# Seven-product feed-forward sets: the last two products exchanged, operand splits in halves of the depth

## The reference, cut to what matters

```
x = x + 0.5 * swiglu_ffn(rmsnorm(x), ffn1 gate, up, down)
x = x + hybrid_mixer(rmsnorm(x), ...)
x = x + 0.5 * swiglu_ffn(rmsnorm(x), ffn2 gate, up, down)
x = rmsnorm(x)

def swiglu_ffn(x, w_gate, w_up, w_down):
    return (silu(x @ w_gate) * (x @ w_up)) @ w_down        # hidden width 2816
```

## Time and profile before

| | us |
|---|---|
| median of three runs | 1777.34 |
| profiled execution | 1777.71 |
| its span | 1775.9 |
| PE busy | 1721.1 (97%) |
| DVE busy | 1010.5 (57%) |
| ACT busy | 704.5 (40%) |
| PE waiting before a product of the seven-product sets (L1600) | 16.2, 14 times |

### The profile page before, as it was taken

How to read it: one execution, slowest core, us unless ns; L and a number is a source line. 1 busy time by engine, 2 the same in 40 slices (tenths; PEclk the granted TensorE clock), 3 DMA queues, 4 the chain that set the end, 5 groups by cost and what they waited for, 6 DMA issues and landing times.

```text
span 1775.9 us, 21351 instructions
## 1 busy us (share of the span) xinstructions
PE 1721.1 (97%) x8703; PEld 1277.9 (72%) x8703; DVE 1010.5 (57%) x1489; ACT 704.5 (40%) x1144; POOL 78.9 (4%) x78
## 2 busy tenths in 40 slices
PE   7999999998999999999999999999999999999998
PEld 6878888885454545454477788898877887788896
DVE  4768865643333333333457866765577457856765
ACT  4556435441111111111335445454355435545453
POOL 0000000000000000000001111100000001111100
PEclk9999999998999999999999999999999999999999
DMA  6222225547999999999947888883303167898781
GB/s 216 94 72 72 95 81 180 193 154 289 421 421 420 421 421 421 420 421 421 372 122 170 213 201 196 179 190 124 119 0 107 49 194 185 192 220 196 166 200 56
DMA packets 117512, 385.74 MB, mean 217 GB/s; under 512 B 7088, under 2 KB 22592, under 8 KB 91424
## 3 DMA queue, kind: packets, MB, share of 16 engines
q1 hardware_dynamic: 88928, 318.33, 46.7%
q0 software_dynamic: 26176, 61.78, 18.9%
q10 hardware_dynamic: 2304, 4.20, 0.6%
HBM read 364.36 MB, written 6.29 MB: 209 GB/s over the span
## 4 chain that ended last, share of the span: by engine, by line
PE 85%; DVE 9%; ACT 5%; issue 1%; DMA 0%; SPq 0%; DVEq 0%; ACTq 0%
PE PS L1491 12%; PE PS L1600 8%; PE PS L1602 8%; PE PS L1601 8%; PE PS L1524 6%; PE PS L1630 6%; PE PS L1632 6%; PE PS L1631 6%; PE PS L1634 3%; PE PS L1636 3%; PE PS L1635 3%; DVE lo L2386 2%; PE PS L1462 2%; PE PS L1463 2%; PE PS L1534 2%; PE PS L1708 2%
## 5 line engine op out<-in xcount | busy, mean ns | idle before, releaser
L2386 DVE TENSOR_TENSOR lo<-raw,hi 128x1024 fp32r<-128x1024 f32 (+2 forms) x273 | 328.1, 1232 | 199.1 <-ACT hi L1939 195.6
L1939 ACT CAST hi<-raw 128x1024 fp32r<-128x1024 f32 (+2 forms) x275 | 282.4, 1066 | 220.9 <-PE PS L1602 142.9
L1600 PE MATMUL PS<-hi,xh_ffn 128*128 128x512 f32 (+1 forms) x320 | 118.5, 370 | 6.3 <-issue 4.0
L1602 PE MATMUL PS<-hi,xl_ffn 128*128 128x512 f32 (+1 forms) x320 | 117.6, 368 | 0.0
L1601 PE MATMUL PS<-lo,xh_ffn 128*128 128x512 f32 (+1 forms) x320 | 117.5, 367 | 0.0
L1491 PE MATMUL PS<-raw,XG 128*64 128x512 f32 x352 | 117.1, 593 | 0.0
L2346 DVE TENSOR_TENSOR HF<-SG,PS 128x512 f32<-128x512 f32 x16 | 17.4, 1090 | 164.8 <-PE PS L1491 164.8
L2361 DVE SCALAR_TENSOR_TENSOR YL<-PS,SM,YH 128x512 fp32r<-128x512 f32 x30 | 21.1, 746 | 138.8 <-ACT YH L1922 138.8
L2369 DVE TENSOR_TENSOR x_sb<-x_sb,PS 128x512 f32<-128x512 f32 x128 | 78.2, 678 | 8.7 <-PE PS L1535 8.7
L1905 ACT COPY HT<-PS 128x512 f32<-128x512 f32 x16 | 9.4, 586 | 175.1 <-PE PS L1500 175.1
L1634 PE MATMUL PS<-xTh,hi 128*128 128x512 f32 x192 | 78.3, 408 | 0.4 <-DVE lo L2386 0.3
(11 more groups left out here) (520 smaller groups left out, 4237.5 us busy)
## 6 DMA issues: line engine op xcount, KB each, us to landing
raw<-in_w_in SPq DMA_DIRECT2D x26, 1024.0 KB, 5.1
rawz<-in_w_down_experts SPq DMA_DIRECT2D x25, 1024.0 KB, 10.9
raw<-in_w_up_experts SPq DMA_DIRECT2D x24, 1024.0 KB, 16.0
raw<-in_w_gate_experts SPq DMA_DIRECT2D x20, 1024.0 KB, 15.5
raw<-in_ffn_w_down SPq DMA_DIRECT2D x20, 1024.0 KB, 6.0
rawz<-in_w_up_experts SPq DMA_DIRECT2D x19, 1024.0 KB, 19.1
raw<-in_w_down_experts SPq DMA_DIRECT2D x16, 1024.0 KB, 12.0
rawz<-in_w_gate_experts SPq DMA_DIRECT2D x16, 1024.0 KB, 13.8
```

Source lines behind the costliest of these rows:

```text
L1600: e.matmul(o, xh[:, k, c], h[:, k, :], start=k == 0 and not more, stop=False, skip_group_check=more)
L1602: x = e.matmul(o, xl[:, k, c], h[:, k, :], start=False, stop=k == 3, skip_group_check=more)
L1939: e.copy(q.hi[:, a:b], q.raw[:, a:b]).then_inc(*a_hi((u, 0) if part == 0 else u))
L2386: e.tensor_tensor(q.lo[:, a:b], q.raw[:, a:b], q.hi[:, a:b].bitcast(F32), ALU.subtract).then_inc(*v_lo(key))
```

## The change

The last two products of a set change places: the lower left one (A22 on T4) is now the sixth and goes onto bank 4 (behind S3's), the end of the chain on bank 0 (S4 on the fourth block) is the seventh. So the hidden-end rows are complete after the sixth product and the hidden-top rows after the seventh; copy R0 (of bank 4 after product 1) takes the place of R4. The transposes of RB now stand before the next set's first product, with `hb` behind the seventh; those of SGT stand behind the next set's first product, with `ht` just ahead of them. The down set's left sums and splits are written at other products.

Every set is worked by halves of the depth. PE runs both row blocks on depths 0 and 1, then both on depths 2 and 3, and signals after the first half. `split_first` writes, directly behind product j, the cast and the rest of the first half of the weights of product j+2; the cast waits for product j's half (`hl_first`). The second half is written where the whole split stood. In the last down product rows 2, 3 come before 0, 1.

```diff
--- before.py
+++ after.py
     def split_to(self, j):
         while self.split < min(j, len(self.units)):
-            if self.halves and self.units[self.split].four:
+            if self.units[self.split].four:
                 u = self.first + self.split
-                self.steps.extend([("hi", u, 0), ("hi", u, 1), ("lo", u, 0), ("lo", u, 1)])
+                if self.rounded:
+                    self.steps.extend([("hi", u, 1), ("lo", u, 1)])
+                else:
+                    self.steps.extend([("hi", u, 0), ("hi", u, 1), ("lo", u, 0), ("lo", u, 1)])
                 self.split += 1
+                self.rounded = False
                 continue
             self.split_hi()
             self.split_lo()
+
+    def split_first(self):
+        u = self.first + self.split
+        if self.split < len(self.units) and self.units[self.split].four and self.units[self.split - 2].by_halves:
+            self.steps.extend([("hi", u, 0), ("lo", u, 0)])
+            self.rounded = True
...
-        self.plan = [self.t3, self.b11, self.b21, self.t2, self.t1, self.b22, self.t4]
-SEVEN = ("S3", "A11", "A12", "S2", "S1", "S4", "A22")
-BANK = (4, 0, 2, 0, 0, 0, 4)
-PAST = {3: 1, 4: 3, 5: 4, 6: 0}
-QUARTER = [(1, 1), (0, 0), (0, 0), (1, 0), (1, 1), (0, 1), (1, 0)]
+        self.plan = [self.t3, self.b11, self.b21, self.t2, self.t1, self.t4, self.b22]
+SEVEN = ("S3", "A11", "A12", "S2", "S1", "A22", "S4")
+BANK = (4, 0, 2, 0, 0, 4, 0)
+PAST = {3: 1, 4: 3, 5: 0, 6: 4}
+QUARTER = [(1, 1), (0, 0), (0, 0), (1, 0), (1, 1), (1, 0), (0, 1)]
...
+    def gates(w, at):
+        return [(w, pre, *at, t) for t in range(2)]
+
     past = None
-    feed.halves = True
     for what in SETS:
         behind = {j: [] for j in range(7)}
         ahead = []
         if past:
-            ahead = turns(*past, (0, 1))
-            behind[0] = [(w, pre, *past, t) for w in ("sgb", "hb") for t in range(2)]
+            ahead = turns(*past, (2, 3))
+            behind[0] = gates("ht", past) + turns(*past, (0, 1))
         if what[0] == "gu":
             p, cut = what[1:]
-            own = {1: ("R1",), 2: ("C11",), 3: ("sg", "R2"), 4: ("R4", "C22"), 5: ("ht",), 6: ("C21",)}
+            own = {1: ("R1",), 2: ("C11",), 3: ("R2", "sg", "R0"), 4: ("C22",), 5: ("C21", "sgb"), 6: ("hb",)}
             for j, ws in own.items():
-                behind[j].extend((w, pre, p, cut, t) for w in ws for t in range(2))
-            if past:
-                behind[0].extend(turns(*past, (2, 3)))
+                for w in ws:
+                    behind[j].extend(gates(w, (p, cut)))
             if (p, cut) == (0, 1):
                 behind[0].extend([("sum", pre, "x", "S1"), ("sum", pre, "x", "S2")] + split_left(pre, "x", "S2"))
                 behind[1].extend(split_left(pre, "x", "S1") + [("sum", pre, "x", "S4")])
                 behind[2].extend(split_left(pre, "x", "S4") + turns(0, 0, (0, 1)))
                 behind[3].extend(turns(0, 0, (2, 3)))
             if p < NS and cut:
-                j = 2 if p else 4
-                behind[j].extend([("sum", pre, p, "S3")] + split_left(pre, p, "S3"))
-                behind[j + 1].extend(split_left(pre, p, "A11"))
+                behind[4].extend([("sum", pre, p, "S3")] + split_left(pre, p, "S3"))
+                behind[5].extend(split_left(pre, p, "A11"))
             past = (p, cut)
         else:
             p = what[1]
-            behind[0].extend(split_left(pre, p, "A12") + turns(*past, (2, 3)))
-            behind[1].extend([("sum", pre, p, "S1"), ("sum", pre, p, "S2")] + split_left(pre, p, "S2"))
-            behind[2].extend(split_left(pre, p, "S1"))
-            behind[3].append(("sum", pre, p, "S4"))
-            behind[4].extend(split_left(pre, p, "S4"))
-            behind[5].extend(split_left(pre, p, "A22"))
-            for j, js in ((1, (1,)), (2, (0,)), (3, (3,)), (4, (4,)), (5, (5, 2)), (6, (6,))):
+            behind[0].extend([("sum", pre, p, "S1"), ("sum", pre, p, "S2")])
+            for j, ws in ((1, ("A12", "S2")), (2, ("S1",)), (3, ("A22",)), (4, ("S4",))):
+                for w in ws:
+                    behind[j].extend(split_left(pre, p, w))
+            for j, js in ((1, (1,)), (2, (0,)), (3, (3,)), (4, (4,)), (5, (5,)), (6, (2, 6))):
                 behind[j].extend(("seven_x", pre, p, q, t) for q in js for t in range(2))
+            behind[2].append(("sum", pre, p, "S4"))
             past = None
         for j in range(7):
             u = feed.take((pre, *what))
             S.extend(ahead if j == 0 else ())
-            S.extend(("seven", (pre, *what), j, t, u) for t in range(2))
+            S.append(("seven", (pre, *what), j, u))
+            feed.split_first()
             S.extend(behind[j])
...
-        for i in range(4):
+            S.extend(turns(*past, (2, 3)))
+        for i in range(4) if ui else (2, 3, 0, 1):
             S.append(("mm", key, ui, i, u))
             if ui:
                 S.append(("ev", key, i))
-            elif i == 1:
-                S.extend([(w, pre, *past, t) for w in ("sgb", "hb") for t in range(2)] + turns(*past, (2, 3)))
+            elif i == 3:
+                S.extend(gates("ht", past) + turns(*past, (0, 1)))
...
+                if j >= len(at_hl) and U[first + j - 2].half and u.n <= U[first + j - 2].n:
+                    u.hl_first = [U[first + j - 2].half]
...
+                for half, t in ((0, 0), (0, 1), (1, 0), (1, 1)):
+                    b = BANK[j] + t
+                    pe.wait_ge(a_hi, u if half else (u, 0))
+                    pe.wait_ge(v_lo, u if half else (u, 0))
+                    if not half:
+                        if not more:
+                            taken(b)
+                        elif key[1] == "s":
+                            pe.wait_ge(v_sum, ("x", key[0], key[2], PAST[j], t))
+                        elif j == 6:
+                            pe.wait_ge(v_ev, ("C22", *at_set(key), t))
+                        else:
+                            pe.wait_ge(a_ev, ({3: "R1", 4: "R2", 5: "R0"}[j], *at_set(key), t))
+                    c = slice(t * 128, t * 128 + 128)
+                    o = PS[:, b, 0:q.n]
+                    for k in (2 * half, 2 * half + 1):
+                        e.matmul(o, xh[:, k, c], h[:, k, :], start=k == 0 and not more, stop=False, skip_group_check=more)
+                        e.matmul(o, xh[:, k, c], l[:, k, :], start=False, stop=False, skip_group_check=more)
+                        x = e.matmul(o, xl[:, k, c], h[:, k, :], start=False, stop=k == 3, skip_group_check=more)
+                    if half:
+                        x.then_inc(*p_mm((key, j, t)))
+                    elif t:
+                        x.then_inc(*p_mm((key, j, "half")))
+                for t in range(2):
+                    b = BANK[j] + t
+                    if key[1] == "s":
+                        freed[b] = [(v_sum, ("x", key[0], key[2], j, t))]
+                    elif j in (2, 5, 6):
+                        freed[b] = [(v_ev, ({2: "C11", 5: "C21", 6: "ht"}[j], *at_set(key), t))]
...
-                for s, k in q.hl_free:
+                for s, k in q.hl_first if part == 0 and q.hl_first else q.hl_free:
...
-            def R4(n, p, cut, t):
-                act.wait_ge(p_mm, ((n, "gu", p, cut), 4, t))
+            def R0(n, p, cut, t):
+                act.wait_ge(p_mm, ((n, "gu", p, cut), 0, t))
                 act.wait_ge(a_ev, ("sg", n, p, cut, t))
                 w = FPARTS[p][cut][1] - FPARTS[p][cut][0]
-                e.copy(RA[t][:, 0:w], PS[:, t, 0:w]).then_inc(*a_ev(("R4", n, p, cut, t)))
+                e.copy(RA[t][:, 0:w], PS[:, 4 + t, 0:w]).then_inc(*a_ev(("R0", n, p, cut, t)))
...
-                r, b = {"C11": (RA, 2), "C22": (RA, 4), "C21": (RB, 4)}[w]
+                r, b = {"C11": (RA, 2), "C22": (RA, 0), "C21": (RB, 4)}[w]
```

More of the change, by code:

```diff
@@ L115, in __init__ @@
         self.key, self.src, self.kc, self.n = key, src, kc, n
-        self.raw = self.hi = self.lo = self.slot = self.done = self.made = self.four = None
+        self.raw = self.hi = self.lo = self.slot = self.done = self.half = self.made = self.four = None
         self.last = False
         self.raw_free, self.hl_free, self.lo_free = [], [], []
+        self.hl_first = None
+        self.by_halves = False
 class Feed:
@@ L1152, in place @@
                 u.hl_free = at_hl[h] if j < len(his) else [U[first + j - len(his)].done]
+        for f in fours.values():
+            for j, q in enumerate(f.plan):
+                if q.by_halves:
+                    q.half = (p_mm, (f.key, j, "half"))
         for group, first, n in ((p1, 0, len(p1)), (p2, first_moe, len(p2)), (p3, first3, len(p3)), (p5, first5, len(p5))):
@@ L1162, in program @@
                     group[j].last = key not in [q.key for q in group[j + 1:]]
[L1163 removed]
+                    group[j].done = (p_mm, (key, ui, 0 if key[0] == "ffn2" and key[1:] in (("g", 0, 0), ("u", 0, 0)) and not (key[1] == "u" and ui) else
```

(26 more changed lines are left out.)

23 lines of the change are left out of this document (10 added, 13 removed).

## The result

| | us |
|---|---|
| kernel before, median of 4 runs on the same chip | 1776.84 |
| changed kernel, median of 4 runs | 1806.09 |
| ratio, with its 95% interval | 1.0164 [1.0146, 1.0181] |
| span of the profiled execution | 1803.4, against 1775.9 |

The change makes the kernel 1.6% slower. Forecast were 1802 us, with a range of 1783 to 1819.

A forecast was written before the change was run, and what follows sets the result against it. PE, busy 97% of the span, bounds the kernel, so its waits are time. Losses (a) to (d) of 41.2 us against 20.0 gained give +21.2; with 3 for the clock, 1777.7 becomes 1802 us, range 1783 to 1819.

The forecast's parts named there:

- What goes: PE's waits for casts and rests of weights in the seven-product sets and first down product: all 20.0 us gone.
- (a): Plain set boundaries: hb or ht stands behind the early rest, so PE's transposes cost 0.7 us each; 4.2 a block.
- (b): Ahead of each down set, left sums also in the queues: the set starts 4.0 us late, twice a block, 8.0.
- (c): In down sets: A12's rest delays product 3 by 1.07 + 0.08, x addition product 5 by 1.9 + 0.08; 6.3 a block.
- (d): Before the last down product: C21's gate, a whole hi and its rest delay hb; PE loses 2.1 us per block.
- (e): PE meets four boundaries inside a product instead of two: taken as 0, upper end 15.7 us.
- (f): Half clock after the four long waits of (b): 3 us, from falls at two of them; bounds 0 and 20.
- The rival that had all four long waits fall: Clock rival: each of the four waits of (b) costs 5.1 us of slower clock, 1819 us; chance 9%.
- Slack wins: Rival: DVE and ACT queues catch up during waits, (a) to (d) cost nothing, only the 20.0 gain remains: 1758 us; 8%.
- both effects cancel: Rival: gains and losses balance, time within 0.2% of the kernel before; chance 4%.
- Short chain: Rival: left sums overlap better, so the 4.0 us of (b) shrink to 0.7: 1786 us; chance 12%.
- Late sum: Rival: T4's DMA takes 5 us longer, product 5 waits 2.1 us in each of 14 sets: 1828 us; 3%.

The follow-up runs named there:

- halves alone: The kernel before, old order and queues, no early split, with each product run and waited for by halves of the depth: 1773.07 us, ratio 0.9972.
- the fill: The changed kernel plus 84 matmuls of no use where PE idles before RB's transposes ahead of down sets and before their fifth product: 1798.08 us, ratio 1.0114.
- 1768.4: Halves alone, plus in each down set the fourth product's addition to x moved ahead of the sum S4 on DVE: 1768.41 us, ratio 0.9947.
- 1764.8: The 1768.4 kernel, plus the sum S3 of each down set written one product earlier: 1764.79 us, ratio 0.9926.

## Why the prediction was right, point by point

**The sum and its sign.** Forecast 1802, measured 1806.1; the forecast mechanism, transposes and products that wait for DVE's late evictions, is the one that the trace shows, and its size agrees but for the clock.

**What goes: right.** Every wait of PE for a cast or a rest of the weights is gone in the sets, and that for the first down product too. Which part of the change does it the prediction left open, and the runs share it out: of 13.5 us of waits for weights halves alone take 7.9 and give 3.9 back at the addition to x; without the early split 5.0 are left in the new order (2.5 for lo, 2.0 for hi, 0.5 for issue), and only the split ahead of the evictions takes these too.

**(a) 0.7 at a boundary: right.** 0.34 us idle, a restart, and a second group that waits in its turn: SGT's transposes at 987.06 take 1.25 instead of 1.03. The run with hb and ht ahead bears the term out with 0.72.

**(b) 4.0 ahead of a down set: right.** C21, LB1l, two rests and hb stand in the counted order: the count put the start of the transposes 3.81 us behind the time at which they could have started, 0.16 of it the end of the last matmul, so 3.65 idle; measured are 3.63, 3.58, 3.67 and 3.58. That chain has a part that is not the early split's: with the split behind the evictions or gone 2.0 to 2.3 us of wait remain ahead of each down set and 1.6 ahead of the last product, since in the new order hb is wanted at once, where it had a whole product before. The prediction had this in its count (of the 4.0, one rest is the split's), but did not set it apart.

**(c) A12 1.07, x addition 1.9: right.** Measured 0.87 and 1.86. **(d) 2.1: near.** 1.64 idle and a restart, and the same with the split behind the evictions, so this term belongs to the new order.

**(e) Boundaries inside a product, taken as 0: right,** of a bound of 15.7: halves alone won 0.7 us more than their waits.

**(f) The clock, 3 us of a bound of 20: the term that was mis-sized.** It is 8.4 us by the fill and 9.5 by the rows. The prediction looked only at the four long waits and took the cost of a short fall, 1.5 us, at two of them. There were five falls of 1.4 to 2.9 us each. Three of the four long waits had half clock at their end or just behind it, once for 6.83 us, and two of the four waits of 1.86 us as well, although 1.75 and 1.75 at 1503.54 had left it at full in the kernel before. The step that failed is that only long waits count; its sign for the profile, "right behind a long wait or nowhere", failed with it. The rival that had all four long waits fall at 5.1 us each put 1819 and was further off, 20 us of clock for 8.4 to 9.5.

The prediction also weighed the rule of the Trainium skill's "TensorE: Matmul & The Clock Gate" (Part 1), that the default is throttled and activity releases it. The trace agrees in that it has two levels, 0.50 and 1.00, and nothing between. The strict form that the prediction gave the rule, a fall at all four long waits, is not borne out: the clock is 1.00 from 1650 to 1660, around the end of the fourth (1652.35).

**The ledger.** ffn1 took 14.6 us more (349.1 us before, from 885.99 to 1235.07; 363.7 after, 884.22 to 1247.93), the rest from there 14.6 more; the part ahead of it 1.8 less, since the stretch of half clock at 386.74 is not there after. Without the clock, ffn1 lost 8.5 and the second block 11.2; the prediction's terms give 20.6 less 10.0 a block, 10.6. So part of the nearness of 1802 is luck: the clock term was 6.5 us too small by the rows, and 1.5 us too much in the other terms and the 1.8 us ahead of the blocks, which was not forecast, made up for half of that.

**Rivals.** Slack wins (1758) and both effects cancel are refuted: transposes wait, and the time grew by 1.6%. Short chain (1786): the waits of (b) are full length. Late sum (1828): no wait for a cast behind T4.

**What stays open.** Why the clock falls behind one wait of 1.86 us and not behind the next was not settled, nor why it falls for 6.83 us once and for 3.41 otherwise. The length of the wait does not decide it: with the split behind the evictions the clock fell just behind a wait of 2.16 us (1513.07) and at none of 2.33 and 2.34 (1104.74 and 1637.99), and with only hb and ht ahead at none of the four of 1.86. A result a few us apart can hold one or two such falls; the last steps of 4.7 and 3.6 us (1773.1, 1768.4, 1764.8) are of that size, and rest on the waits that went as much as on the time.

## What to carry to other kernels

Work that is brought forward in an engine's strict queue costs twice if it has to wait for its own input: its length is added to all that stands behind it, and so is its pause; ask of each piece not only whether it is in time but who stands behind it while it waits. Before slack is bought for the piece that PE waits for, look whether the queue behind it has a pause at all: in a stretch where DVE has none, a removed wait comes back at the next piece, and only a changed order of pieces or less work wins. Idle time of a busy PE has to be priced with the slower clock at and behind it: here 32.7 us of waits cost 8.4 more.

## What the runs showed of the hardware that I had not expected

An idle of 1.86 us, with no other wait of PE for 11 us ahead of it, was followed by half the clock, 1.3 to 1.4 us later, in two of four places (from 1008.98 and 1681.41), while at the four of 3.6 us it came in three. Useless matmuls in the idle time kept the clock up and cost nothing that shows: 84 of them, 19 us of PE work in waits that were there anyway, made the kernel 8.4 us faster.
